# Layer two's up product with two direct pairs in place of three, and an earlier third operand split at both down products

## The chip, the cores and the metric

The kernel runs on 1 core of one Trainium2 chip. The metric is device time in microseconds (us), lower is better. A core has five engines that run their own instruction streams and wait for each other through semaphores: TensorE (matmul), VectorE, ScalarE, GpSimd, and SyncE (SP), which here only issues DMAs. 16 DMA engines move data between HBM and the on-chip memory.

## The reference, cut to what matters

One inference step of a two-layer decoder for 1024 prompt tokens and 64 sample tokens (8 sequences of 8), width 1024. Layer 1 has an attention mixer, layer 2 a pooling mixer; each layer ends with the same MLP:

```python
def _sq_relu_mlp(x, w1, w2):                 # w1 (1024, 4096), w2 (4096, 1024)
    return jnp.square(jax.nn.relu(x @ w1)) @ w2
...
xp = xp + _rms(_sq_relu_mlp(_rms(xp, gl[2]), mlp_w1[l], mlp_w2[l]), gl[3])
xs = xs + _rms(_sq_relu_mlp(_rms(xs, gl[2]), mlp_w1[l], mlp_w2[l]), gl[3])
```

Here xp are the prompt rows and xs the sample rows, l is the layer and gl its norm gains. Everything is float32. The change touches the MLPs of both layers, mostly the up product `x @ w1` of layer 2.

## The kernel before, in words

**Three passes.** TensorE takes fp32r operands, which are rounded. To keep float32 precision every operand is split in a high part (ScalarE, a copy to fp32r) and a low part (VectorE, raw minus high), and each product is made of three matmuls: high by high, high by low, low by high.

**The up product.** w1's 4096 columns are 32 tiles of 128, taken as 16 pairs (i = 0 to 15). A pair can be done in two ways. *Direct*: two tiles, each 8 row blocks by 3 passes by 3 token chunks (384, 384 and 320 wide), 72 matmuls (`up`, L1909, recorded as L1918; `up_chunk`, L1922, for the first two tiles). *By seven products* (Winograd's form of Strassen's scheme, `LateUp` for layer 2 and `SevenUp` for layer 1): P1 to P7, each 4 row blocks by 3 passes by 2 chunks of 272, 24 matmuls, in the order P1, P6, P2, P7, P5, P4, P3 (`product`, L2595, recorded as L2604), 168 a pair. The seven products need four sums of quarters of the tokens, made once (`token_sum`, `token_hi`, `token_lo`, L2878 to L2907, numbers 1 to 4, each 128 by 2176; sum 2 needs sum 1, sum 4 needs sum 2), four sums of weight quarters for each pair on GpSimd (`sum_weights`), the high and low parts of the seven weight operands (`w_split_hi`, `w_split_lo`, index q in the order of the products), and VectorE and ScalarE to take the results from PSUM (`take_out` makes U2, U3, C22, C21, C12 after P6, P7, P5, P4, P3; P7 waits for U2, P4 for U3, P3 for C22).

In layer 2 the first `FIRST` = 3 pairs (`TILES` = 6 tiles) are direct and 13 are by products. The direct tiles are there since the token sums are made while they run: `token_sum(1)` can only start when the normalised tokens have all been transposed. GpSimd adds up the first pair's weight quarters at the same time. VectorE's program is `dve_up` of `LateUp`, written out by hand, and ScalarE's is `act_up`; engines take their instructions strictly in that order. The places in PSUM go round by `bank`; `wait_place` has the waits for them.

**Between up and down.** For each pair VectorE also makes five sums of hidden rows (`combine_s`, L2485) and five of w2 rows (`combine_t`, L2499, from `one_w2`, a single buffer), which SP stores to HBM (`store_s`, `store_t`). `load_w2(i)` fills the buffer for pair i after `combine_t(i-1)`.

**The down product** is the same scheme on a larger scale: seven products M7, M1, M4, M5, M3, M2, M6, each of 8 chunks g of 24 matmuls, 512 wide (`down_part`, L1957; four of the products have 4 more for the sample rows, L1975). Chunk g's operands are loaded from HBM (`load_operands(g)`, which waits until the low parts of chunk g-2 are made, since raw buffers are two), split by ScalarE (`split_operands_hi`) and by VectorE (`split_operands_lo`, a_lo L1748 and b_lo L1751). Before the change VectorE's order at the end of the up product is: low parts of chunks 0 and 1, `combine_s(15)`, `combine_t(15)`, then low parts of chunk 2, 3, ... (with sample splits after chunk 3). SP's order is: operands 0 and 1, `store_s(14)`, operands 2, `store_t(14)`, `load_w2(15)`, operands 3, `store_s(15)`, `store_t(15)`, operands 4, ...

## Time and profile before

| | before |
|---|---|
| median of 3 runs | 2125.13 us (2122.82 to 2130.16) |
| profiled execution | 2128.65 us, span of its trace 2126.9 us |
| TensorE busy | 2048.9 us, 96% |
| VectorE busy | 1310.8 us, 62% |
| ScalarE busy | 922.2 us, 43% |
| GpSimd busy | 356.8 us, 17% |
| mean granted TensorE clock | 0.986 of 2.4 GHz |
| chain that ended last | TensorE 64%, DMA 6%, VectorE 5% |

The profile is of one execution. Its span goes from the first to the last instruction; 1.7 us of the profiled execution lie around it. An operation's time is from its start to its end, and neighbours on one engine overlap a little, so the step from start to start is the better price of one in a row. "<-DVE t_w_lo L1684" behind an operation names what the engine waited for before it; the number ahead of it is the idle time. Matmuls are pipelined: the time of one says less than that of a row of them.

### The profile page before, as it was taken

What the parts mean: (1) busy time and instruction counts of PE and PEld (TensorE: products, weight loads), DVE (VectorE), ACT (ScalarE), POOL (GpSimd) and SP (SyncE); (2) the same over time, 40 slices, a digit from 0 to 9 for tenths busy, and PEclk for the clock granted to TensorE, in tenths of its full rate; (3) what the DMA queues carried; (4) which work ended last, traced back from release to release, by engine and by line L of the source; (5) the groups of instructions that cost most, each with busy time, mean ns of one, the idle gap of its engine ahead of it and who ended that gap; (6) DMA issues with size and microseconds to landing.
All of it is one profiled execution on the core that took longest, in us unless ns stands there. A gap on an engine that the chain in (4) does not pass through costs nothing.

```text
span 2126.9 us, 34612 instructions
## 1 busy us (share of the span) xinstructions
PE 2048.9 (96%) x13923; PEld 1837.2 (86%) x13923; DVE 1310.8 (62%) x1888; ACT 922.2 (43%) x1591; POOL 356.8 (17%) x375
## 2 busy tenths in 40 slices
PE   7999999999999999999899999989999998999998
PEld 7999877777778899999788878889999997888876
DVE  5121187666556778787645467669687776444475
ACT  5111397645445444444333346454444444333343
POOL 1000131000053333331000013222232320000011
PEclk9999999999999999999999999999999999999999
DMA  5321211099522577777876542444677769664464
GB/s 168 96 74 51 101 70 35 1 355 366 160 97 84 203 260 244 258 246 285 299 252 228 165 159 97 132 135 141 208 256 243 252 223 341 230 223 160 159 221 139
DMA packets 206235, 394.39 MB, mean 185 GB/s; under 512 B 19005, under 2 KB 101109, under 8 KB 197756
## 3 DMA queue, kind: packets, MB, share of 16 engines
q1 hardware_dynamic: 199884, 387.46, 53.4%
q10 hardware_dynamic: 6192, 4.72, 0.7%
q8 instruction: 111, 1.82, 0.4%
q14 instruction: 48, 0.39, 0.1%
HBM read 273.12 MB, written 119.24 MB: 184 GB/s over the span
## 4 chain that ended last, share of the span: by engine, by line
PE 64%; DMA 6%; DVE 5%; POOL 2%; issue 2%; SPq 1%; ACT 1%; POOLq 0%; DVEq 0%; ACTq 0%
PE ps L1957 26%; PE ps L2604 25%; PE ps L4135 4%; PE ps L1975 3%; PE ps L1918 2%; DMA sa_vb_even<-cache_b_v 1%; DMA sa_vb_odd<-cache_b_v 1%; PE ps L4055 1%; DMA l_b_raw<-scratch_t_ops 1%; PE ps L1927 1%; SPq L675 1%; PE ps L4028 1%; DVE l_t_sum L2892 1%; DMA wo_raw<-attn_w_out 1%; DMA l_w_raw<-mlp_w 1%
## 5 line engine op out<-in xcount | busy, mean ns | idle before, releaser
L1957 PE MATMUL ps<-t_b_hi,t_a_hi 128*128 128x512 f32 x448 | 178.2, 398 | 7.3 <-DVE t_b_lo L1751 6.3
L1957 PE MATMUL ps<-l_b_hi,l_a_hi 128*128 128x512 f32 x448 | 175.7, 392 | 8.0 <-DVE l_b_lo L1751 7.0
L1957 PE MATMUL ps<-t_b_lo,t_a_hi 128*128 128x512 f32 x448 | 175.4, 391 | 0.0
L1957 PE MATMUL ps<-t_b_hi,t_a_lo 128*128 128x512 f32 x448 | 175.3, 391 | 0.0
L1957 PE MATMUL ps<-l_b_lo,l_a_hi 128*128 128x512 f32 x448 | 175.2, 391 | 0.0
L1957 PE MATMUL ps<-l_b_hi,l_a_lo 128*128 128x512 f32 x448 | 175.2, 391 | 0.0
L1530 POOL TENSOR_SCALAR stats<-stats 128x1 f32<-128x1 f32 x63 | 32.6, 518 | 785.7 <-ACT t_junk_y L1524 611.0
L1748 DVE TENSOR_TENSOR l_a_lo<-l_a_raw,l_a_hi 128x1024 fp32r<-128x1024 f32 x56 | 68.6, 1225 | 144.3 <-ACT l_a_hi L2634 144.3
L2634 ACT ACTIVATE l_a_hi<-l_a_raw 128x1024 fp32r<-128x1024 f32 x56 | 59.4, 1061 | 219.0 <-PE ps L1975 140.0
L1748 DVE TENSOR_TENSOR t_a_lo<-t_a_raw,t_a_hi 128x1024 fp32r<-128x1024 f32 x56 | 68.6, 1224 | 133.7 <-ACT t_a_hi L2634 133.7
L2634 ACT ACTIVATE t_a_hi<-t_a_raw 128x1024 fp32r<-128x1024 f32 x56 | 59.4, 1061 | 195.8 <-PE ps L1975 135.7
L2604 PE MATMUL ps<-u_x_sum_hi,u_w_hi 128*128 128x272 f32 x512 | 107.4, 288 | 2.7 <-DVE u_h L2466 2.7
L1957 PEld LDWEIGHTS ps<-l_b_hi,l_a_hi 128*128 128x128 f32 x448 | 84.7, 189 | 28.0 <-DVE l_b_lo L1751 7.4
L1957 PEld LDWEIGHTS ps<-t_b_hi,t_a_hi 128*128 128x128 f32 x448 | 84.8, 189 | 27.8 <-DVE t_b_lo L1751 6.7
L2604 PE MATMUL ps<-u_x_sum_lo,u_w_hi 128*128 128x272 f32 x512 | 106.9, 288 | 0.0
L1957 PEld LDWEIGHTS ps<-t_b_hi,t_a_lo 128*128 128x128 f32 x448 | 84.7, 189 | 17.9
L1957 PEld LDWEIGHTS ps<-l_b_hi,l_a_lo 128*128 128x128 f32 x448 | 84.7, 189 | 17.8
L1957 PEld LDWEIGHTS ps<-l_b_lo,l_a_hi 128*128 128x128 f32 x448 | 84.7, 189 | 17.5
L1957 PEld LDWEIGHTS ps<-t_b_lo,t_a_hi 128*128 128x128 f32 x448 | 84.9, 189 | 17.2
L985 ACT ACTIVATE pa_probs<-pa_probs,pa_least 128x257 f32<-128x257 f32 (+9 forms) x128 | 80.5, 630 | 20.2 <-DVE pa_least L1023 19.1
L2604 PE MATMUL ps<-m_xT_hi,l_w_hi 128*128 128x272 f32 x416 | 86.1, 288 | 0.0
L2604 PE MATMUL ps<-m_xT_lo,l_w_hi 128*128 128x272 f32 x416 | 85.9, 288 | 0.0
(390 smaller groups left out, 5693.3 us busy)
## 6 DMA issues: line engine op xcount, KB each, us to landing
scratch_s_ops<-u_s SPq DMA_DIRECT2D x16, 1280.0 KB, 4.8
scratch_t_ops<-u_t SPq DMA_DIRECT2D x16, 1280.0 KB, 5.7
t_a_raw<-scratch_s_ops SPq DMA_DIRECT2D x40, 512.0 KB, 3.9
t_b_raw<-scratch_t_ops SPq DMA_DIRECT2D x40, 512.0 KB, 4.8
scratch_t_ops<-l_t SPq DMA_DIRECT2D x16, 1280.0 KB, 5.5
scratch_s_ops<-l_s SPq DMA_DIRECT2D x16, 1280.0 KB, 4.6
l_a_raw<-scratch_s_ops SPq DMA_DIRECT2D x40, 512.0 KB, 3.9
l_b_raw<-scratch_t_ops SPq DMA_DIRECT2D x40, 512.0 KB, 4.8
```

The lines of the kernel that those rows point to most:

```text
L675: sp.dma_start(self.values[b % 2][:, 2 * x:2 * x + 2, :].rearrange("p e c -> p (e c)"), cache_pair(self.cache["b_v"], b, x)).then_inc(self ...
L985: nc.scalar.activation(row, row, ACT.Exp, bias=least[:, i, d:d + 1], scale=-1.0, accum_out=den[:, i, d:d + 1]).then_inc(exped, 1)
L1530: nc.gpsimd.tensor_scalar(self.ms[:, col], self.ms[:, col], EPS, None, ALU.add).then_inc(core.shifted, 1)
L1748: nc.vector.tensor_tensor(sb.a_lo[g % 3][:], sb.a_raw[:, g % 2], sb.a_hi[g % 3][:].bitcast(F32), ALU.subtract).then_inc(self.operand_lo, 1)
L1918: mm = self.nc.tensor.matmul(out, a[:, k, :], b_[:, k, c], start=(k == 0 and x == 0), stop=(k == KT - 1 and x == 2))
L1927: mm = self.nc.tensor.matmul(out, a[:, k, :], b_[:, k, c], start=(k == 0 and x == 0), stop=(k == KT - 1 and x == 2))
L1957: mm = self.nc.tensor.matmul(self.core.ps[:, self.BANK[idx] + tp, :], a[s][:, kk, tp * P:(tp + 1) * P], w[s][:, kk, :], start=(c == 0 and ...
L1975: mm = self.nc.tensor.matmul(self.core.ps[:, self.SAMPLE_BANK[idx], :], self.xT_lo[:, k % KT, first:first + P], w[s][:, kk, :], start=(k = ...
L2604: mm = self.nc.tensor.matmul(self.core.ps[:, b + j, 0:self.CHUNK], w[:, k, :], t[:, k, j * self.CHUNK:(j + 1) * self.CHUNK], start=(x in s ...
L2634: self.nc.scalar.activation(sb.a_hi[g % 3][:], sb.a_raw[:, g % 2], ACT.Copy).then_inc(self.operand_hi, 1)
L2892: sub(t[n], a, b, how).then_inc(self.x_summed_last, 1)
L4135: op = nc.tensor.matmul(out_ps(j)[:, n * 512:(n + 1) * 512], a, w[:, n * 512:(n + 1) * 512], start=(i == 0 and x == 0), stop=(i == KT - 1 ...
```

## The change

Four edits:

1. Layer 2's up product: `FIRST` from 3 to 2, so four direct tiles and 14 pairs by products. The banks of the products go round in another order (6, 4, 2, 0), the two weight buffers change places, the first product loses its wait for ScalarE's relu, and the first down chunk waits for an earlier result.
2. VectorE's and ScalarE's programs in the up head are written anew for four tiles: `split_lo(3)` right behind the first token sum, the weight parts 0 to 3 between token sums and low parts, `combine_s(1)` and `combine_t(1)` left to the first pair by products.
3. SP, both layers: `load_operands(3)` goes ahead of `load_w2(15)`.
4. VectorE, both layers: `split_operands_lo(2)` goes ahead of `combine_t(15)`; the loops that follow start from 3.

```diff
--- before.py
+++ after.py
@@ -2236,8 +2236,9 @@
                 self.load_operands(sp, 2)
             if i >= 1:
                 self.store_t(sp, i - 1)
+                if i == PAIRS - 1:
+                    self.load_operands(sp, 3)
                 self.load_w2(sp, i)
-        self.load_operands(sp, 3)
         self.store_s(sp, PAIRS - 1)
         self.store_t(sp, PAIRS - 1)
 
@@ -2567,6 +2568,7 @@
         self.split_operands_lo(dve, 1)
         for piece in range(5):
             self.combine_s(dve, PAIRS - 1, piece)
+        self.split_operands_lo(dve, 2)
         for piece in range(5):
             self.combine_t(dve, PAIRS - 1, piece)
 
@@ -2690,8 +2692,9 @@
 
 
 
-    FIRST = 3
+    FIRST = 2
     SLOTS = 5
+    PLACE_BANK = (6, 4, 2, 0)
     TILES = 2 * FIRST
     LEAD = 0
     ORDER = [(i, x) for i in range(FIRST, PAIRS) for x in (1, 6, 2, 7, 5, 4, 3)]
@@ -2718,7 +2721,7 @@
         self.x_sum[1] = [xT_hi[:, 0:k, H:], xT_lo[:, 0:k, H:]]
         self.t_sum = {n: at(f"t_sum{n}", o + lo, [P, k, H])[:] for n, o in places.items()}
         self.t_sum[1] = at("t_sum1", LateMap.TOKENS, [P, k, H])[:]
-        weights = (LateMap.WEIGHTS_EVEN, LateMap.WEIGHTS_ODD)
+        weights = (LateMap.WEIGHTS_ODD, LateMap.WEIGHTS_EVEN)
         self.w_sum = [at(f"w_sum{s}", o, [P, 3, k, P]) for s, o in enumerate(weights)]
         self.w_sum_lo = [at(f"w_sum_lo{s}", o, [P, 3, k, P], F32R) for s, o in enumerate(weights)]
         self.e1 = [at(f"w_e1_{s}", o + 6144, [P, KT, P]) for s, o in enumerate(weights)]
@@ -2821,8 +2824,9 @@
             if i == PAIRS - 1:
                 self.load_operands(sp, 2)
             self.store_t(sp, i - 1)
+            if i == PAIRS - 1:
+                self.load_operands(sp, 3)
             self.load_w2(sp, i)
-        self.load_operands(sp, 3)
         self.store_s(sp, PAIRS - 1)
         self.store_t(sp, PAIRS - 1)
 
@@ -2925,7 +2929,7 @@
 
     def act_up(self, act):
 
-        order = {1: 2, 2: 4, 3: 3}
+        order = {1: (2,), 2: (4, 3)}
         for n in range(self.TILES):
             if n + 2 < self.TILES:
                 self.split_hi(act, n + 2)
@@ -2933,41 +2937,35 @@
                 for q in range(4):
                     self.w_split_hi(act, q)
             self.hidden(act, n)
-            if n in order:
-                self.token_hi(act, order[n])
+            for x in order.get(n, ()):
+                self.token_hi(act, x)
         self.token_hi(act, 1)
         super().act_up(act)
 
     def dve_up(self, dve):
 
         self.token_sum(dve, 1)
+        self.split_lo(dve, 3)
+        self.token_sum(dve, 2)
         for piece in range(5):
             self.combine_t(dve, 0, piece)
-        self.token_sum(dve, 2)
-        self.split_lo(dve, 3)
         self.token_sum(dve, 4)
         self.token_lo(dve, 2)
-        self.split_lo(dve, 4)
+        self.token_sum(dve, 3)
+        for q in range(2):
+            self.w_split_lo(dve, q)
+        self.token_lo(dve, 4)
+        for q in range(2, 4):
+            self.w_split_lo(dve, q)
         for piece in range(5):
             self.combine_s(dve, 0, piece)
-        self.token_lo(dve, 4)
-        self.token_sum(dve, 3)
-        self.split_lo(dve, 5)
-        for piece in range(5):
-            self.combine_t(dve, 1, piece)
         self.token_lo(dve, 3)
-        for piece in range(5):
-            self.combine_s(dve, 1, piece)
-        for q in range(4):
-            self.w_split_lo(dve, q)
         self.token_lo(dve, 1)
         super().dve_up(dve)
 
     def wait_place(self, pe, i, x):
 
-        if i == self.FIRST and x == self.P1:
-            pe.wait_ge(self.relu_done, 3 * (self.TILES - 1))
-        elif i == self.FIRST and x == self.P6:
+        if i == self.FIRST and x == self.P6:
             pe.wait_ge(self.relu_done, 3 * self.TILES)
         super().wait_place(pe, i, x)
 
@@ -2992,7 +2990,7 @@
             if tp == 0:
                 pe.wait_ge(self.c11_taken, self.PAST["c11_taken"] + PAIRS - self.FIRST)
             if tp == 2:
-                pe.wait_ge(self.added, self.PAST["added"] + self.nth_added(PAIRS - 1, self.C21))
+                pe.wait_ge(self.added, self.PAST["added"] + self.nth_added(PAIRS - 2, self.C12))
         elif idx == self.M1:
             pe.wait_ge(self.added, self.PAST["added"] + 5 * (PAIRS - self.FIRST))
         else:
@@ -3869,7 +3867,7 @@
             m0.w_split_lo(dve, 7)
             m0.w_split_lo(dve, 8)
             m0.dve_up(dve)
-            for s in range(2, 40):
+            for s in range(3, 40):
                 m0.split_operands_lo(dve, s)
                 m0.down_slot(dve, s)
                 if s == 26:
@@ -3981,7 +3979,7 @@
             m1.split_lo(dve, 2)
             dve.wait_ge(x3_stored, 16 * NT)
             m1.dve_up(dve)
-            for s in range(2, 56):
+            for s in range(3, 56):
                 m1.split_operands_lo(dve, s)
                 m1.down_slot(dve, s)
                 if s == 42:
```

## Rows read from the trace of the kernel before

**Rows 1.** Chain of waits by time: start, us, what.

```profile
1016.83 40.98 PE ps L1957 x168
...
1446.65 4.11 DVE l_t L2499 x5
...
1456.75 38.94 PE ps L1918 x216
...
1505.08 6.24 PE ps L2604 x48
...
1511.36 244.25 PE ps L2604 x1944
...
1830.27 5.44 PE ps L1957 x24
```

**Rows 2.** TensorE's timeline: start, us, operation, idle time before it, releaser.

```profile
1456.75 1.27 PE L1918 MATMUL ps<-m_xT_hi,t_w_hi 128*128 128x384 f32 x3 [3.08 <-DVE t_w_lo L1684]
```

**Rows 3.** Stretches: length, busy PE, PEld, DVE, ACT, POOL, granted clock, DMA share, GB/s.

```profile
1015.00:1016.00 1.00, 0.00 (x0) 0.00 (x0) 1.00 (x2) 1.00 (x3) 0.00 (x0) 0.79 0.92 389
...
1455.00:1456.00 1.00, 0.00 (x0) 0.00 (x0) 1.00 (x2) 0.41 (x1) 0.00 (x0) 0.95 0.77 158
...
1462.00:1463.00 1.00, 1.00 (x5) 1.00 (x5) 1.00 (x1) 1.00 (x1) 0.00 (x0) 0.64 0.00 0
```

**Rows 4.** The page's costliest groups: the down product's first pass in layer 2.

```profile
L1957 PE MATMUL ps<-l_b_hi,l_a_hi 128*128 128x512 f32 x448 | 175.7, 392 | 8.0 <-DVE l_b_lo L1751 7.0
```

**Rows 5.** VectorE's timeline at the start of the down products.

```profile
1011.40 3.10 DVE L2499 TENSOR_TENSOR u_t<-u_w_raw 128x512 f32<-128x512 f32 x5 [3.93 <-DMA u_w_raw<-mlp_w]
...
1026.39 1.22 DVE L1751 TENSOR_TENSOR t_b_lo<-t_b_raw,t_b_hi 128x1024 fp32r<-128x1024 f32 x1
...
1775.27 3.19 DVE L2485 TENSOR_TENSOR l_s<-l_h 128x512 f32<-128x512 f32 x5 [0.36 <-ACT l_h L2449]
```

**Rows 6.** GpSimd's timeline in layer 2's up head.

```profile
1444.33 3.47 POOL L2262 TENSOR_TENSOR l_w_sum<-l_w_e,l_w_sum 128x512 f32<-128x512 f32 x1
```

**Rows 7.** VectorE's timeline in layer 2's up head.

```profile
1470.22 2.42 DVE L2892 TENSOR_TENSOR l_t_sum<-m_xT_hi 128x2176 f32<-128x2176 f32 x1
...
1477.50 1.23 DVE L1684 TENSOR_TENSOR t_w_lo<-t_raw,t_w_hi 128x1024 fp32r<-128x1024 f32 x1
...
1481.80 2.43 DVE L2907 TENSOR_TENSOR l_x_sum_lo<-l_t_sum,l_x_sum_hi 128x2176 fp32r<-128x2176 f32 x1
...
1484.14 3.10 DVE L2485 TENSOR_TENSOR l_s<-l_h 128x512 f32<-128x512 f32 x5
...
1487.15 0.69 DVE L2301 TENSOR_TENSOR l_w_e_lo<-l_w_e,l_w_hi 128x512 fp32r<-128x512 f32 x1
...
1504.22 0.71 DVE L2466 TENSOR_TENSOR l_h<-l_first,ps 128x544 f32<-128x544 f32 x1
```

**Rows 8.** ScalarE's timeline in layer 2's up head.

```profile
1498.13 2.01 ACT L2900 ACTIVATE m_xT_hi<-l_t_sum 128x2176 fp32r<-128x2176 f32 x1
...
1500.05 0.61 ACT L2292 ACTIVATE l_w_hi<-l_w_sum 128x512 fp32r<-128x512 f32 x1
```

**Rows 9.** ScalarE's timeline at the start of the down products.

```profile
1014.05 1.06 ACT L2634 ACTIVATE t_a_hi<-t_a_raw 128x1024 fp32r<-128x1024 f32 x1 [6.26 <-DMA t_b_raw<-scratch_t_ops]
...
1024.15 1.06 ACT L2634 ACTIVATE t_a_hi<-t_a_raw 128x1024 fp32r<-128x1024 f32 x1 [6.02 <-DMA t_b_raw<-scratch_t_ops]
...
1777.71 1.04 ACT L2635 ACTIVATE l_b_hi<-l_b_raw 128x1024 fp32r<-128x1024 f32 x1
```

**Rows 10.** SP's queue in layer 1.

```profile
1000.73 0.43 SPq L2201 DMA_DIRECT2D u_w_raw<-mlp_w  x1
...
1014.53 0.33 SPq L2205 DMA_DIRECT2D scratch_t_ops<-u_t  x1
...
1016.86 0.37 SPq L1655 DMA_DIRECT2D t_a_raw<-scratch_s_ops  x1
```

**Rows 11.** A stretch of layer 1, columns as in rows 3.

```profile
1014.05:1024.15 10.10, 7.32 (x21) 5.84 (x22) 8.62 (x10) 4.09 (x6) 0.00 (x0) 0.66 1.02 412
```

## The prediction

> **What bounds the kernel now.** The page first: TensorE is busy for 96% of the span, and the chain of waits lies on it for 64%, mostly in L1957 and L2604. A change on other engines pays only where TensorE stands still. The chain in order of time and TensorE's timeline show three such places that the change touches. All times are us from the span's start.
>
> At layer 2's up head the six direct tiles come before the pairs of seven products. Tile 3 waits for its low part, which stands in VectorE's program behind the first token sum, `combine_t(0)` and the second token sum. TensorE idles 3.08, from 1453.67 to 1456.75 [rows 1, 2]. The granted clock fell to 1.2 GHz at 1455.9, in that idle time, and came back at 1462.7 (a slice at 0.95 and one at 0.64 give the moments [rows 3]), so 6.0 of tile 3 ran at half pace and 3.0 more were lost. Tiles 3 to 5 took 38.94; less 3.0, a tile is 12.0. Product P7 of the first pair starts at 1505.08, its last four products are done 12.3 later, at 1517.4, and 1944 matmuls take 244.25 without a pause, which is 21.1 for a pair of 168 [rows 1].
>
> At each down product chunk 2 waits for its low parts: 7.0 idle in layer 2 and 6.3 in layer 1 [rows 4]. These stand behind `combine_t(15)`, which waits for the last w2 load [rows 5]. Chunk 2 starts at 1016.83, so chunk 1 ended at 1010.5. Seven chunks then take 40.98 where 168 matmuls at 5.44 for 24 take 38.1 [rows 1]: the other 2.9 is the clock, which fell 5 into the idle time, at 1015.6 [rows 3]. Layer 2 repeats it: chunk 1 ends at 1781.5, chunk 2 starts at 1788.54, seven take 40.83, and the clock fell 2 into the idle time. Chunk 4 thus starts at 1016.83 + 40.98 - 27.2 = 1030.6, and at 1788.54 + 40.83 - 27.2 = 1802.2.
>
> **The up head, VectorE.** I follow its new program from the same start, 1436.3; nothing ahead of it changes. First token sum, beside GpSimd's weight sums: to 1446.6. `split_lo(3)`: 1.1 alone. It meets GpSimd's last weight sum, which runs to 1447.8 [rows 6]; `combine_t` took 4.1 in this place against 3.1 free of it [rows 1, 5], so I add 1.0: 1448.7. That is 5 ahead of the end of tile 2, so tile 3 starts at 1453.7 at full clock and ends at 1465.7. Gain so far: 3.1 + 3.0 = 6.1.
>
> From here each step of a token sum is 2.4 (the third sum's three take 7.3), a low part 2.3 and `combine_s` 3.0, from start to next start [rows 7]. Second sum 4.8, `combine_t(0)` 3.0, fourth sum 4.8, low part of sum 2 2.3, third sum 7.3: to 1471.0. ScalarE's program has the high part of sum 3 ahead of the first weight parts: 1.9 for it, 0.6 for the weight [rows 8], 0.2 of handing over, to 1473.7. VectorE waits for that, then `w_split_lo(0)` takes 0.6 [rows 7]. The first product can start at 1474.4, and TensorE has stood idle for 8.7. This is a new wait, and what is queued behind it on VectorE is all that the next products need.
>
> VectorE goes on: `w_split_lo(1)` 0.6, low part of sum 4 2.3, two weight parts 1.2, `combine_s(0)` 3.0, low parts of sums 3 and 1 4.7, `w_split_lo(4)` 0.6, to 1486.8. Then U2 is taken, and P7 starts 0.86 after that begins, as before [rows 1, 7]: 1487.6. The three products between take 9.05 at full clock, or 12 if the first 6 run at half, and end by 1486.4: the clock falls where VectorE is later anyway. I cost that at nothing; without the cover it costs 3.0.
>
> **Sum of the up head.** P7 at 1487.6, four products 12.3, one more pair 21.1: 1521.0, against 1517.4, so 3.6 later. By its parts: two direct tiles -23.9, stall and slow clock before tile 3 -6.1, a pair +21.1, stall before P1 +8.7, from P1 to P7 +3.8 (13.2 in place of 9.4). Behind that: the next loads go out after `store_s(0)`, whose sum is ready at 1481.5; GpSimd's weight sums then run at about 1491 to 1498, beside VectorE's takes for P4 and P3. The trace has no such overlap there; the nearest row is the wait of 0.3 before P4 in the old first pair, inside the 12.3. Bounds: 0.3 less, and 1.5 more (two small operations held up by 1.0 each, less slack). I take nothing. The other end of the head: were P1 not held up, P7 would still wait for VectorE's 47.8 of work, until 1485.0, so the head can be at best 1.0 later. The new order of banks frees P1 from a wait for ScalarE's relu; P1 is later than that anyway, so it is worth nothing. Two fewer direct weight loads and the earlier bank wait of the first down chunk free only idle time.
>
> The Trainium skill (SBUF — State Buffer, "Who interferes with whom") says that a VectorE operation with two SBUF inputs and a GpSimd operation that reads SBUF exclude each other for a whole instruction. The trace shows less in this stretch: both took about 3.4 side by side, where 2.4 and 1.7 alone would add up to 4.1. By the rule `split_lo(3)` waits until 1447.8 and ends at 1449.0, not 1448.7, and the sum is 0.3 later.
>
> **The down start, both layers.** The low parts of chunk 2 now come right after `combine_s(15)`. Layer 2: `combine_s` ends at 1778.5 [rows 5], the high parts at 1778.8 [rows 9], the low parts at 1780.9, before chunk 1 ends at 1781.5. So chunk 2 starts with no wait. But what stays behind `combine_t(15)` is now chunk 3, and `combine_t` is itself later: `load_w2(15)` is moved behind `load_operands(3)`, which waits on SP for the low parts of chunk 1. The queue is full through this stretch (DMA share 1.02 at 412 GB/s [rows 11]), and transfers land in the order of issue, w2 at 1011.4 and operands 3 at 1014.05 [rows 5, 9]. So they change places: w2 lands at 1014.05, and in layer 2 at 1786.4. `combine_t` 3.1 and chunk 3's low parts 2.3 give 1019.4 and 1791.8. Chunk 2 ends at 1010.5 + 5.44 = 1015.9 and at 1786.9: new stalls of 3.5 and 4.9.
>
> Chunk 4 comes next. `load_operands(4)` is no longer held by the low parts of chunk 2 but stands on SP's queue behind `store_t(15)`, which waits for `combine_t(15)`. The store goes out at 1017.2, not 1014.53 [rows 10], and at 1789.6, not 1786.2. While the queue still has the `s` store to move, that costs nothing, and operands 4 land at 1024.15 as before [rows 9], in layer 2 at 1796.5; where it runs dry first, up to 1.0 and 1.6. I take 0.7 and 1.2. From landing to the end of the low parts was 3.46 [rows 5, 9], so chunk 4 can start at 1028.3 and 1801.2. Chunk 3, from 1019.4 and 1791.8 at a slow clock, ends by 1027.7 and 1800.0: covered. The gain is 1030.6 - 1028.3 = 2.3 in layer 1 and 1802.2 - 1801.2 = 1.0 in layer 2: of 9.2 and 9.7, most comes back as the stalls before chunks 3 and 4. Bounds: 3.0 and 2.2 if operands 4 land as before; below nothing if the clock falls twice.
>
> **Sum.** +3.6 - 2.3 - 1.0 = +0.3. The profiled execution took 2128.65 (span 2126.9); it would be 2128.95. The median of the runs is 2125.13, 3.5 below it, with 7.3 between the ends of three runs; on the median: 2125.4.
>
> **Rivals.** (1) Slower, by the clock. If the clock doesn't fall in the stall before chunk 3, chunk 3 ends at 1024.9, TensorE idles again until 1028.3, the clock falls in that second stall and chunk 4 runs slow on the path: 2.7 to 3.0 lost in each layer, which turns -3.3 into +2.4. With the overlap with GpSimd in the head (+1.5) this is +7.5: 2132.6. For it: both idle times of [rows 3], and layer 2's, were followed by a slow stretch. Against: the clock fell within 2.3 of the start in two of the three, so the first stall should take it. It decides from the point where chunk 3 runs at full clock. The Trainium skill (TensorE: Matmul & The Clock Gate, "HAM oscillation") has this as half the throttled time, paid again at each wait that is long enough; it speaks against cutting one stall in two.
>
> (2) Faster, by the queue. If latency and not bytes sets when operands 4 land, their earlier issue (by at most 1.9, from 1016.86 to 1014.95) counts, and w2 isn't delayed. Then the down starts gain 4.9 and 4.1; with +3.6 the sum is -5.4: 2119.7. Against it: the DMA share of 1.02.
>
> (3) The head does what its title says: P1 starts at tile 3's end because weight parts precede the sums. The programs as written don't do that before the third sum; it would give 2.6 at most: 2122.8.
>
> **How the numbers follow.** Forecast, within 4 of no change: 0.70. Rival 1: 0.14. Rival 2: 0.06. Rival 3: 0.05. Something else: 0.05. A measurement of this kernel can tell about 0.3% from no change, 6.4. Faster by more than that needs rival 2 and luck: 0.06; slower, most of rival 1: 0.12; within: 0.82. The range reaches past rival 2 and to most of rival 1: 2119.0 to 2132.0.
>
> **What would show it.** Right: TensorE idle 8 to 9 before the first product of layer 2's pairs and 1 to 4 before its P7; no wait at chunk 2 of either down product, 3.5 and 4.9 at chunk 3 with `b_lo` as releaser, 0 to 3 at chunk 4. Wrong: no stall before P1 (the head is off by up to 2.6), w2 landing at its old time (the swap), a slow clock in chunk 4 (rival 1).

## The result, and the profile after

The changed kernel takes 2137.51 us (median of 9 runs, 2132.52 to 2145.12), the kernel before 2125.07 on the same chip. The ratio is 1.0053, 95% interval 1.0041 to 1.0065: 11.3 us slower, between 8.7 and 13.8. Forecast was no change, with the range up to 2132.0.

The profiled execution took 2132.52 (span 2130.7), only 3.9 more than that of before. It is the fastest of its nine, and before's lies 3.6 above the median of its runs, so the two spans must not be subtracted. I compare the changed places instead: the layer 1 down product from its first matmul to its first sample matmul (L1957, L1975), layer 2's up product from tile 0 to its end, and the layer 2 down product as the first. The first and last times of these lines give them.

| us | down start, layer 1 | up, layer 2 | down start, layer 2 | sum |
|---|---|---|---|---|
| before | 58.1 | 336.6 | 58.7 | 453.4 |
| after | 60.3 | 343.0 | 57.5 | 460.8 |
| after, minus before | +2.2 | +6.4 | -1.2 | +7.4 |
| forecast | -2.3 | +3.6 | -1.0 | +0.3 |

The page's groups of after, as [rows 4]:

```profile
L1957 PE MATMUL ps<-t_b_hi,t_a_hi 128*128 128x512 f32 x448 | 178.5, 398 | 8.5 <-DVE t_b_lo L1751 7.5
L1957 PE MATMUL ps<-l_b_hi,l_a_hi 128*128 128x512 f32 x448 | 175.5, 392 | 6.5 <-DVE l_b_lo L1751 6.3
...
L2606 PE MATMUL ps<-m_xT_hi,l_w_hi 128*128 128x272 f32 x448 | 93.5, 290 | 9.9 <-DVE l_w_e_lo L2302 8.8
```

The down product waits as long as before (7.5 and 6.3, against 6.3 and 7.0), and a wait of 8.8 is new. TensorE's timeline of after has the single stalls, as [rows 2] (the idle time stands in the brackets):

```profile
1017.94 0.50 PE L1957 MATMUL ps<-t_b_hi,t_a_hi 128*128 128x512 f32 x1 [4.03 <-DVE t_b_lo L1751]
...
1028.74 0.63 PE L1957 MATMUL ps<-t_b_hi,t_a_hi 128*128 128x512 f32 x1 [3.44 <-DVE t_b_lo L1751]
...
1473.01 0.82 PE L2606 MATMUL ps<-m_xT_hi,l_w_hi 128*128 128x272 f32 x2 [8.76 <-DVE l_w_e_lo L2302]
...
1486.15 0.62 PE L2606 MATMUL ps<-l_x_sum_hi,l_w_hi 128*128 128x272 f32 x2 [2.46 <-DVE l_h L2467]
...
1498.10 0.49 PE L2606 MATMUL ps<-m_xT_hi,l_w_hi 128*128 128x272 f32 x2 [1.17 <-DVE l_h L2467]
...
1796.05 0.50 PE L1957 MATMUL ps<-l_b_hi,l_a_hi 128*128 128x512 f32 x1 [4.08 <-DVE l_b_lo L1751]
...
1805.61 0.50 PE L1957 MATMUL ps<-l_b_hi,l_a_hi 128*128 128x512 f32 x1 [2.20 <-DVE l_b_lo L1751]
```

Chunks 3 and 4 stall in both layers; in the head P1, P7 and P3. I had not forecast the last. The chain of waits of after says where it comes from:

```profile
1480.13 0.34 SPq L2791
...
1481.94 1.25 SPq L2182
...
1483.24 7.39 DMA l_w_e<-mlp_w
...
1490.79 1.29 POOL l_w_sum L2258
...
1494.69 1.25 POOL l_w_sum L2263
...
1496.03 0.10 DVE l_w_e_lo L2302
...
1497.24 0.73 DVE l_h L2467
```

SP issues the store of `combine_s(0)` (L2791) and only then the weight loads of the second pair. They land at 1490.63, GpSimd's four sums run to 1495.94, and then comes a step of VectorE that I had not seen. Its timeline:

```profile
1445.15 2.31 DVE L1684 TENSOR_TENSOR t_w_lo<-t_raw,t_w_hi 128x1024 fp32r<-128x1024 f32 x1
...
1485.29 0.72 DVE L2467 TENSOR_TENSOR l_h<-l_first,ps 128x544 f32<-128x544 f32 x1
...
1496.03 0.69 DVE L2302 TENSOR_TENSOR l_w_e_lo<-l_w_e,l_w_hi 128x512 fp32r<-128x512 f32 x1 [4.35 <-POOL l_w_sum L2263]
...
1497.24 0.72 DVE L2467 TENSOR_TENSOR l_h<-l_h,ps 128x544 f32<-128x544 f32 x1
```

`w_split_lo(7)`, the low part of the second pair's P1, uses raw weights and no sum. But it overwrites them in place, so it waits until GpSimd has read them for all four sums. It stands ahead of the take of C22 (1497.24), and P3 waits for C22.

The clock, in stretches of after (columns as in rows 3):

```profile
1015.00:1016.00 1.00, 0.00 (x0) 0.00 (x0) 1.00 (x3) 0.00 (x0) 0.00 (x0) 1.00 0.23 88
...
1020.00:1021.00 1.00, 1.00 (x4) 0.78 (x3) 0.97 (x2) 0.00 (x0) 0.00 (x0) 0.50 0.55 166
...
1030.00:1031.00 1.00, 1.00 (x4) 0.79 (x3) 1.00 (x2) 0.91 (x2) 0.00 (x0) 0.50 0.66 168
...
1487.00:1488.00 1.00, 1.00 (x6) 1.00 (x6) 0.87 (x2) 0.91 (x2) 0.00 (x0) 0.50 1.15 348
```

It is at 1.2 GHz after chunk 3's stall, again after chunk 4's in layer 1, and again after P7's. In the first row the DMA queue moves 88 GB/s: it has run dry, since SP issued nothing between 1006.3 and 1015.64.

### The profile page after: what moved, and what is told of

Read it like the earlier page. It is cut to its first block and busy times, and to the rows that moved or that the text cites. A ratio compares the mean times of both kernels' runs of the same rounds, so it can differ in the third digit from the quotient of the medians.

```text
span 2130.7 us, 34702 instructions
## 1 busy us (share of the span) xinstructions
PE 2042.7 (96%) x13947; PEld 1831.3 (86%) x13947; DVE 1321.3 (62%) x1898; ACT 926.9 (44%) x1593; POOL 362.2 (17%) x380
## 5 line engine op out<-in xcount | busy, mean ns | idle before, releaser
L1957 PE MATMUL ps<-t_b_hi,t_a_hi 128*128 128x512 f32 x448 | 178.5, 398 | 8.5 <-DVE t_b_lo L1751 7.5
L1957 PE MATMUL ps<-l_b_hi,l_a_hi 128*128 128x512 f32 x448 | 175.5, 392 | 6.5 <-DVE l_b_lo L1751 6.3
L1957 PE MATMUL ps<-t_b_lo,t_a_hi 128*128 128x512 f32 x448 | 175.8, 393 | 0.0
L1957 PE MATMUL ps<-t_b_hi,t_a_lo 128*128 128x512 f32 x448 | 175.5, 392 | 0.0
L1957 PE MATMUL ps<-l_b_lo,l_a_hi 128*128 128x512 f32 x448 | 175.0, 391 | 0.0
L1957 PE MATMUL ps<-l_b_hi,l_a_lo 128*128 128x512 f32 x448 | 174.9, 390 | 0.0
L1957 PEld LDWEIGHTS ps<-t_b_hi,t_a_hi 128*128 128x128 f32 x448 | 84.8, 189 | 29.5 <-DVE t_b_lo L1751 8.3
L1957 PEld LDWEIGHTS ps<-l_b_hi,l_a_hi 128*128 128x128 f32 x448 | 84.5, 189 | 26.8 <-DVE l_b_lo L1751 7.1
L2606 PE MATMUL ps<-m_xT_hi,l_w_hi 128*128 128x272 f32 x448 | 93.5, 290 | 9.9 <-DVE l_w_e_lo L2302 8.8
L1957 PEld LDWEIGHTS ps<-t_b_hi,t_a_lo 128*128 128x128 f32 x448 | 85.0, 190 | 18.1
L1957 PEld LDWEIGHTS ps<-l_b_hi,l_a_lo 128*128 128x128 f32 x448 | 84.5, 189 | 17.8
L1957 PEld LDWEIGHTS ps<-t_b_lo,t_a_hi 128*128 128x128 f32 x448 | 84.9, 189 | 17.2
L1957 PEld LDWEIGHTS ps<-l_b_lo,l_a_hi 128*128 128x128 f32 x448 | 84.4, 188 | 17.4
L2606 PE MATMUL ps<-m_xT_lo,l_w_hi 128*128 128x272 f32 x448 | 93.0, 289 | 0.0
```

The lines of the kernel that those rows point to most:

```text
L1957: mm = self.nc.tensor.matmul(self.core.ps[:, self.BANK[idx] + tp, :], a[s][:, kk, tp * P:(tp + 1) * P], w[s][:, kk, :], start=(c == 0 and ...
L2606: mm = self.nc.tensor.matmul(self.core.ps[:, b + j, 0:self.CHUNK], w[:, k, :], t[:, k, j * self.CHUNK:(j + 1) * self.CHUNK], start=(x in s ...
```

## The experiments

A ratio of 1.001 is 2.1 us. "In the trace" is the sum of the three changed places less before's 453.4; "measured" is the timed ratio.

| kernel | in the trace | measured (95%) |
|---|---|---|
| changed | +7.4 | +11.3 (+8.7 to +13.8) |
| changed, second profile | +6.6 | |
| down edits alone | +0.5 | +3.8 (+0.4 to +7.0) |
| head alone | +6.2 | +8.5 (+5.7 to +11.3) |
| second loads first | +10.5 | +11.9 (+8.3 to +15.3) |
| weights first | +5.3 | +8.1 (+4.9 to +11.1) |
| early low part, three pairs | -3.2 | -3.4 (-5.7 to -1.1) |
| late w2 sums, three pairs | -5.7 | -6.4 (-9.4 to -3.2) |
| take before split | +6.4 | +4.9 (+1.9 to +7.9) |
| down, VectorE edit alone | +0.3 | -1.3 (-4.0 to +1.7) |
| operands first, three pairs | -8.4 | -8.5 (-11.7 to -5.1) |
| both fixes, three pairs | -10.3 | -10.8 (-14.7 to -7.2) |
| two pairs, eased program | +1.4 | +3.0 (0.0 to +6.2) |

The trace's figure lies inside the interval for every kernel but the changed one, where it is 1.3 short of its lower end. The places left out take 1669 to 1681 us in these traces, in no order that goes with an edit.

Two cautions. First, one trace is one execution. Where a place is not edited, it still varies: the head with three direct pairs and the old order takes 336.6, 335.5, 335.5, 336.6 and 335.4 in five traces, the old down start 58.1, 57.1 and 58.5 in layer 1 and 58.7, 57.8 and 59.4 in layer 2. A difference of 1 us between two rows therefore says nothing. Second, "down edits alone", "head alone", "second loads first" and "weights first" were timed on another chip than the runs below them, each against the kernel before on its own chip. A difference of two timed rows across that line can hold a difference of the chips.

### The two halves of the change

Before with edits 3 and 4 only, and the changed kernel with these two undone.

> The kernel before with the down edits alone (operands 3 ahead of the last w2 load on SP, low parts of chunk 2 ahead of combine_t(15), both layers). Theory A, the head holds the loss: the two down starts cancel, as in the one trace of the changed kernel (chunk 4 ran 1.6 us later in layer 1, 1.6 us earlier in layer 2, counted from the end of chunk 1), so within 2.5 us of before. Theory B, the down starts hold it because chunk 4 now stalls too and the clock falls twice in each: 5 to 8 us slower than before. The prediction's own sum would be 3.3 us faster.

> The changed kernel with the down edits undone, so two direct pairs and the new programs of the up head alone. Theory A: the head loses the 3.6 us of the prediction and 2.7 more, the stall before P3 that the trace of the changed kernel shows, plus the slow clock after the stall before P7, so 6 to 12 us slower than before. Theory B: 3 to 5 us slower.

The head gives +6.2 in the trace and +8.5 timed, as theory A had it (6 to 12); the down edits give +0.5 and +3.8. They add up. The 3.8 lies between the two theories on the down starts (within 2.5, or 5 to 8), and its interval reaches into both; the trace is on the side of the first. The down edits alone show the changed kernel's stalls, 4.20 and 3.47 in layer 1, 4.44 and 1.69 in layer 2: so they owe nothing to the new head. They bring +2.4 in layer 1 and -0.8 in layer 2. In the trace of the head alone the waits are shared out otherwise than in the changed kernel: 1.42 before P7 with the clock at 2.4 GHz behind it, and 3.08 before P3 with 3.4 us at 1.2 GHz behind it. The head takes 344.7 there.

### The second pair's loads first

```diff
                 self.load_w2(sp, i + 1)
+                sp.wait_ge(self.up_ready, self.TILES)
+                self.load_e0(sp, first + 1)
+                self.load_e1(sp, first + 1)
                 self.store_s(sp, i)
-        sp.wait_ge(self.up_ready, self.TILES)
-        self.load_e0(sp, first + 1)
-        self.load_e1(sp, first + 1)
```

> The changed kernel with the weight loads of the second pair ahead of store_s(0) on SP's queue, so that they go out when the fourth tile ends and not after combine_s(0). If the stall before the first pair's P3 comes from VectorE waiting in w_split_lo(7) for GpSimd's weight sums, and these for late loads, that stall goes and the time falls by 2 to 4 us against the changed kernel. The rival: GpSimd's sums now run beside VectorE's token sums and low parts and slow those (they took 3.4 us side by side where 2.4 alone), P7 comes 3 us later and the time stays or rises by up to 2 us.

The stall before P3 is gone, and nothing is won. TensorE's timeline, and then VectorE's and GpSimd's:

```profile
1480.89 0.82 PE L2606 MATMUL ps<-m_xT_hi,l_w_hi 128*128 128x272 f32 x2 [9.35 <-DVE l_w_e_lo L2302]
...
1496.22 0.49 PE L2606 MATMUL ps<-l_x_sum_hi,l_w_hi 128*128 128x272 f32 x2 [3.41 <-DVE l_h L2467]
```

```profile
1482.45 3.50 DVE L2911 TENSOR_TENSOR l_x_sum_lo<-l_t_sum,l_x_sum_hi 128x2176 fp32r<-128x2176 f32 x1
...
1481.94 1.73 POOL L2263 TENSOR_TENSOR l_w_sum<-l_w_e,l_w_sum 128x512 f32<-128x512 f32 x1
```

GpSimd's sums now fall into VectorE's work between P1 and P7. The low part of sum 4 takes 3.50 in place of 2.42, a weight part 1.76 in place of 0.69, and P7 is 15.3 behind P1, not 13.1. The rival of the expectation holds: in the stretch where VectorE is the bound, GpSimd costs what it saves later. The head is 344.2 against 343.0. The rest of the +10.5 lies in layer 2's down start (59.2 against 57.5), which this edit doesn't touch.

### The weight parts ahead of the third token sum

`w_split_hi(0..3)` on ScalarE ahead of the high parts of sums 4 and 3, and on VectorE:

```diff
-        self.token_sum(dve, 3)
         for q in range(2):
             self.w_split_lo(dve, q)
+        self.token_sum(dve, 3)
         self.token_lo(dve, 4)
```

> The changed kernel with the four high weight parts on ScalarE ahead of the high parts of sums 4 and 3, and the two low weight parts on VectorE ahead of the third token sum. The stall of 8.8 us before P1 goes. If VectorE's whole work up to U2 sets the head, P7 moves by only the 2.6 us that VectorE waited, and a stall of 6 to 9 us appears before P7 (or before P6 or P2, at a low part) in its place: 2 to 4 us faster than the changed kernel. If the stall before P1 is itself the cost, 8 us or more faster.

```profile
1472.10 0.79 PE L2606 MATMUL ps<-l_x_sum_hi,l_w_hi 128*128 128x272 f32 x2 [6.93 <-ACT l_h_sample L2848]
...
1481.36 0.49 PE L2606 MATMUL ps<-l_x_sum_hi,l_w_hi 128*128 128x272 f32 x2 [0.67 <-DVE l_h L2467]
...
1493.64 0.49 PE L2606 MATMUL ps<-m_xT_hi,l_w_hi 128*128 128x272 f32 x2 [3.03 <-DVE l_h L2467]
```

Timed, this is 3.2 better than the changed kernel, inside the expected 2 to 4, but in the trace the head is only 0.9 shorter. P1 starts at tile 3's end, and P6 waits 6.9 for ScalarE's relu of tile 3, which stands behind the high part of sum 3. P7 comes 51.2 behind tile 0, not 53.9: 2.7 earlier, the 2.6 that VectorE had waited. But P3 now waits 3.03, not 1.17, with a slow clock behind it (1494.3 to 1497.6), which takes most of it back. VectorE's work up to P7 was the bound, as expected, and not the stall before P1. Another 1.5 of the trace's gain is layer 1's down start, where the edit does nothing. There a stall of 2.47 before chunk 4 was followed by full clock, the only stall above 2.27 in the down starts and heads of these traces that was:

```profile
1028.26 0.50 PE L1957 MATMUL ps<-t_b_hi,t_a_hi 128*128 128x512 f32 x1 [2.47 <-DVE t_b_lo L1751]
...
1029.00:1030.00 1.00, 1.00 (x6) 0.78 (x6) 1.00 (x2) 1.00 (x3) 0.00 (x0) 1.00 0.68 70
```

### The take of C22 ahead of the in-place low part

VectorE's step 4 makes no weight part, step 5 takes C22 and then makes parts 7 and 8.

> The changed kernel with one move on VectorE: the low part of the eighth weight operand (which waits for all of GpSimd's sums of the second pair) behind the take of C22, not ahead of it. Theory (that wait holds up C22, so TensorE idles ahead of P3 and its clock falls there): no idle time ahead of P3, 1.1 to 2.6 us faster than the changed kernel, so 8.7 to 10.2 slower than the kernel before. Rival (the clock falls anyway, from the stalls before P1 and P7): under 0.5 us of difference in the head.

```profile
1474.04 0.82 PE L2606 MATMUL ps<-m_xT_hi,l_w_hi 128*128 128x272 f32 x2 [8.78 <-DVE l_w_e_lo L2302]
...
1487.19 0.49 PE L2606 MATMUL ps<-l_x_sum_hi,l_w_hi 128*128 128x272 f32 x2 [1.07 <-DVE l_h L2467]
```

No wait before P3. The head takes 339.9, not 343.0: 3.1 less, of which 1.2 is that wait and the rest the slow stretch behind P7, which is missing too. P7 still comes 13.15 after P1, but with 1.07 of idle time ahead of it, since the products before it ran at half pace until 1480.3 (6.2 behind P1, in the changed kernel 3.1); after 1.07 the clock stayed at 2.4 GHz. So 1.2 is owed to the edit, and the rest to where the clock happened to come back. Timed, it is 6.4 better than the changed kernel, so the expected 8.7 to 10.2 over before was too much: +4.9. The sum of the three places is only 1.0 below the changed kernel's, since layer 2's down start is 1.7 longer here. Where the other 5 of the timed difference come from isn't shown.

### Two direct pairs with an eased program

The last two edits together, and the low part of sum 1 behind the take of U2.

> The changed kernel with its head's three waits eased: weight parts 0 to 3 of the first product ahead of the third token sum on both engines, the low part of token sum 1 behind the take of U2, the low part of the eighth weight operand behind the take of C22. Theory (VectorE's 47.8 of work up to P7 is what two direct pairs can't cover, so even a better order wins at most 1 or 2): P1 without a wait, P6 held to about 1476, P7 at 1483 in place of 1487.6, no wait before P3; 5 to 8 faster than the changed kernel, still 2 to 6 slower than the kernel before. Rival (only the order was wrong, not the count of direct tiles): no slower than the kernel with both down edits alone, ratio 1.002 or below.

The head takes 336.3, against 336.6 before and 343.0 changed: TensorE waits 6.93 once, before P6, and nowhere after, up to the down product. Timed, it is +3.0, inside the expected 2 to 6, but the rival's mark (a ratio of 1.002 or below, no slower than the down edits alone) is met too: 1.0014, and +3.0 against +3.8. The head's trace is on the rival's side. The order made the loss, and the count of direct tiles costs nothing that can be seen; this order gains nothing either, and no other was tried. My bound in the prediction ("at best 1.0 later") was passed by 1.3: it counted 47.8 of VectorE's work ahead of P7, and here the low part of sum 1, 2.4 of it, stands behind the take of U2.

### The low part of tile 3, with three direct pairs

```diff
         self.token_sum(dve, 1)
+        self.split_lo(dve, 3)
         for piece in range(5):
             self.combine_t(dve, 0, piece)
         self.token_sum(dve, 2)
-        self.split_lo(dve, 3)
```

> The kernel before with one move on VectorE in layer 2's up head: the low part of tile 3 right behind the first token sum, ahead of the first w2 sums and the second token sum (nothing else, three direct pairs stay). Theory (the stall of 3.1 ahead of tile 3 and the 3.0 of slow clock behind it are on the path, and nothing else waits for VectorE's order there): no idle time ahead of tile 3, clock full through the direct tiles, later work of VectorE covered; 6 us faster than the kernel before. Rival (VectorE's program to the first P7 has no slack, or tile 4 stalls in its place): tile 4's or 5's low part comes late by as much, the gain is below 2.

A gain of 3.4 of the 6.1 (4.3 in the head's trace), between the theory's 6 and the rival's 2. The stall and slow clock at tile 3 are gone, but VectorE's program is full: tile 5 waits for its low part by 1.36, and P7 by 0.68. Neither is followed by a slow clock. 4.3 and these 2.0 come to 6.3, so the price of 6.1 was right. The slow clock at tile 3 was also dearer in before's profile than in most: it came back 6.0 behind the stall's end there, but 3.7 to 3.8 behind it in three of the four other traces with that stall.

### The down start: VectorE's edit alone

> The kernel before with the down edit on VectorE alone (low parts of chunk 2 ahead of the last w2 sums), SP's order as before: w2 lands ahead of operands 3. Theory (w2 and operands 3 change places in a full queue): w2 lands at 1011.4 as before, operands 3 at 1014; chunk 3 stalls by 2 to 3 in place of 3.5 to 4.1, the store of w2 sums and operands 4 go out 1.5 to 2 earlier than with both edits, so chunk 4 waits less; 2 to 6 us faster than the kernel with both down edits. Rival (the clock decides, it falls in whichever stall comes): same stalls within 1, no difference.

```profile
1020.15 0.50 PE L1957 MATMUL ps<-t_b_hi,t_a_hi 128*128 128x512 f32 x1 [1.75 <-DVE t_b_lo L1751]
...
1031.17 0.79 PE L1957 MATMUL ps<-t_b_hi,t_a_hi 128*128 128x512 f32 x1 [5.29 <-DVE t_b_lo L1751]
```

Chunk 3 stalls less, as expected, since operands 3 and w2 stand in another order; chunk 4 stalls more (5.29 against 3.44), but only because chunk 3 is done earlier. Operands 4 land 25.8 behind the product's start, with both down edits 28.0, and chunk 4 begins 29.3 and 31.5 behind it. So in layer 1 the swap of w2 and operands 3 costs 2.0 (down start 58.5 against 60.5). In layer 2 it is the other way round (58.6 against 57.9), and in the table's +0.3 the head, which neither run edits, hides the difference (336.6 against 335.5). Timed, this kernel is 5.1 better than with both down edits, as the theory had it, but the two were timed on different chips and their intervals overlap. The traces show 1.3 of the 5 in the two down starts; the rest stays open.

### The down start: the w2 sums late

Low parts of chunks 2 and 3 ahead of `combine_t(15)`; SP's order operands 3, w2, `s`, operands 4, 5, `t`. Then once more, with operands 4 ahead of the `s` store:

```diff
+        self.load_operands(sp, 4)
         self.store_s(sp, PAIRS - 1)
-        self.load_operands(sp, 4)
         self.load_operands(sp, 5)
         self.store_t(sp, PAIRS - 1)
```

> The kernel before with another down start in both layers: low parts of chunks 2 and 3 ahead of the last w2 sums on VectorE, and on SP operands 3 ahead of the last w2 load, operands 4 and 5 ahead of the last store of w2 sums. Theory (each stall at a down start is VectorE's program order or the DMA queue's order, the change only moved it from chunk 2 to chunks 3 and 4, each time with a slow clock behind it): no wait over 1 us at chunks 2 to 5, no slow clock, 8 to 9 us gained in each layer, 15 to 18 together. Rival (the DMA queue is full and sets the pace, the bytes can't land in time whatever the order): stalls of 2 to 4 us stay at chunks 3 to 5 and the gain is below 6.

> The kernel before with the down start of the run on late w2 sums, but operands 4 on SP ahead of the last store of hidden sums (order: operands 3, last w2 load, operands 4, store of hidden sums, operands 5, store of w2 sums). Theory (the queue is full from 1005 to 1027, so what stands ahead of operands 4 in bytes sets chunk 4's stall of 4.6): operands 4 land 1.79 MB earlier, 4.4 us at 412 GB/s, no stall over 1 at chunks 2 to 5, no slow clock; 4.6 + 4.8 of stalls and some 4 of slow clock less than the run on late w2 sums had, so 14 to 18 us faster than the kernel before. Rival (another chunk or another wait takes the stall's place): under 9 us faster than the kernel before.

TensorE's timeline of the first, a stretch of it in which operands 4 are under way, and the timeline of the second:

```profile
1027.28 0.79 PE L1957 MATMUL ps<-t_b_hi,t_a_hi 128*128 128x512 f32 x1 [4.64 <-DVE t_b_lo L1751]
...
1011.00:1023.78 12.78, 11.63 (x52) 9.30 (x50) 9.00 (x12) 4.09 (x7) 0.00 (x0) 1.00 1.04 406
```

```profile
1033.05 0.79 PE L1957 MATMUL ps<-t_b_hi,t_a_hi 128*128 128x512 f32 x1 [3.21 <-DVE t_b_lo L1751]
...
1799.86 0.50 PE L1957 MATMUL ps<-l_b_hi,l_a_hi 128*128 128x512 f32 x1 [3.06 <-DVE l_b_lo L1751]
```

One stall per layer in place of the changed kernel's two, before chunk 4 in both runs (4.64 and 4.84 in the first, 3.21 and 3.06 in the second), each with a slow stretch. In the first run the bytes set it: the queue moves 406 GB/s without a gap, VectorE is idle ahead of operands 4 and makes their low parts as soon as ScalarE has made the high ones. In the second run 1.79 MB fewer stand ahead of operands 4, and in layer 1 they land 18.7 behind the product's start, not 23.1: 4.4 earlier, just as expected. The stall shrinks by only 1.4 and 1.8, because now VectorE's order is in the way. Its timeline in the second run, layer 1, where operands 4 land at 1026.26:

```profile
1023.96 3.09 DVE L2502 TENSOR_TENSOR u_t<-u_w_raw 128x512 f32<-128x512 f32 x5
1026.98 2.49 DVE L1788 TENSOR_TENSOR m_xT_lo<-u_h_sample,m_xT_lo 128x512 fp32r<-128x512 f32 x4
1029.50 1.23 DVE L1769 TENSOR_TENSOR u_h_sample<-u_h_sample 128x1024 f32<-128x1024 f32 x1
1030.64 1.22 DVE L1748 TENSOR_TENSOR t_a_lo<-t_a_raw,t_a_hi 128x1024 fp32r<-128x1024 f32 x1
```

`combine_t(15)` and the sample splits stand ahead of chunk 4's low parts, and VectorE has no idle time between 1021.7 and 1033.0. Chunk 3 was done at 1029.84. ScalarE has the high parts ready by 1028.3, so with the low parts right behind them chunk 4 could have started some 3 earlier (an estimate from these rows; no run tried it). Both runs gained less than I expected: 6.4, not 15 to 18, and 8.5, not 14 to 18. In the first the rival holds, that bytes set the pace. In the second the rival of its own expectation holds: another wait takes the stall's place.

### Both fixes with three direct pairs

> The kernel before (three direct pairs) with the early low part of tile 3 and the down start with operands first. Theory (the two places are independent): the sum of the two, 17 to 24 us faster than the kernel before. Rival (VectorE or the queue couples them): less than the larger of the two alone plus 1.

The two places are nearly independent: 3.4 and 8.5 give 11.9, measured 10.8, at a median of 2114.97; in the traces 3.2 and 8.4 give 11.6, measured 10.3. The rival's 9.5 at most lies inside the timed interval, so a small coupling isn't excluded. The gain is less than the 17 I expected, as each part was. It beats both kernels.

### The changed kernel, once more

> The changed kernel as it is, for another profile of it: its first profile was taken of its fastest execution, 5 below its median. Theory (the granted clock falls after some short stalls in some executions and not in others): an execution near 2137 shows a slow stretch, or a longer wait, at a place of the up head or the down starts where the first profile had none, and the rest of the trace agrees within 1. Rival (executions differ outside the changed places): the head from tile 3 to the end of the up product takes 343 again and the difference lies elsewhere.

This execution took 2134.99. Head 343.1, down starts 59.9 and 57.0: within 0.5 of the first profile, and the other 3 us lie outside of the changed places. The rival holds: executions differ elsewhere, and one span says nothing on 5 us.

## Why the prediction was wrong, point by point

In the trace the sum is 7.1 above the forecast: 2.8 behind P7, 4.5 in layer 1's down start, less 0.2 in layer 2's. What failed is a wait that I didn't follow (P3), the clock behind two stalls that I forecast but didn't price (P7, chunk 4 of layer 1), and the landing of operands 4 in layer 1.

**The head up to P7: right.** Tile 0 starts at 1432.3, 1.5 ahead of before's. With that shift I had P1 at 1472.9 and P7 at 1486.1; they started at 1473.01 and 1486.15. The stall of 8.7 measured 8.76. `split_lo(3)` took 2.31 beside GpSimd's sum, 1.1 more than alone, where I had added 1.0. The slow clock behind P1's stall was hidden. The Trainium skill's exclusion rule (SBUF — State Buffer, "Who interferes with whom"), which would have made it 0.3 more, can't be told apart here. One reading beside it was wrong: I took 1.7 for GpSimd's weight sum alone, but that row lies beside work of VectorE. With VectorE idle it takes 1.28 in the trace of after, so 2.4 and 1.3 one after the other give 3.7, against the 3.4 of both side by side.

**Behind P7: the step that failed.** I wrote "Bounds: 0.3 less, and 1.5 more … I take nothing". From P7's start to the end of the up product (1775.3 by the last time of its line) 289.15 went by; before took 265.3 (1505.08 [rows 1] to 1770.4), and with one more pair, 21.1, 286.4 was due. Of the 2.8, 1.2 is the stall before P3. I had timed GpSimd's sums right, at 1491 to 1498, but asked only whether they slow VectorE's takes, not who waits for them. The in-place low part does, and the run with the take first shows it: with the take of C22 ahead of that part the wait before P3 is gone. The other 1.6 is the clock: P7's stall of 2.46 was followed by 3.4 at half pace (from 1486 on slices at 0.68, 0.50, 0.50 and 0.62; 3.4 at half pace lose 1.7). I had forecast 1 to 4 of idle time there and put no price on its clock. With these, +3.6 becomes +6.4, as measured. In the run with the head alone the same two terms are shared out otherwise (3.08 before P3 and the slow stretch behind that) and make 4.5.

**The down start, layer 1: wrong by 4.5.** Seen from the product's start, chunk 3 began at 20.5 (forecast 19.9) and chunk 4 at 31.3 (forecast 28.8; 31.1 before). Between them lies operands 4's landing: 27.8 after the start, where I took 24.65 + 0.7, so 2.5 too early. The failed step is "where it runs dry first, up to 1.0": against before they land 3.2 later. SP held the queue for `combine_t(15)` until 1015.64; all that was issued had landed by then (DMA share 0.23), and behind the restart two slices moved at only 215 and 166 GB/s (1019 to 1021). The other part is the clock. It fell behind the stall before chunk 3 (at 1018.7), came back at 1022.1, and fell again behind the stall before chunk 4 (at 1029.0): 3.4 at half pace, 1.7 lost. The first slow stretch cost nothing, since chunk 3 was done before operands 4 had landed. This has the outcome of rival 1, but not its condition and not its price: rival 1 let chunk 3 run at full clock and put 2.7 to 3.0 on the second fall. My argument against it, that the first stall takes the fall, doesn't exclude a second one. I had given it 0.14 in both layers together; the second fall came in layer 1 here and in both layers in three runs (second loads first, take before split, eased program). The Trainium skill (TensorE: Matmul & The Clock Gate, "HAM oscillation") has half the throttled time as the loss, paid again at each wait that is long enough; the trace agrees, with 1.7 of 3.4 lost and the second fall 10.3 us behind the first.

**Layer 2: right, with some luck.** -1.2 against -1.0; chunk 4 began 30.1 behind the product's start, forecast 30.7. But the same down code gave 57.0 to 59.2 in seven traces and the old one 57.8 to 59.4 in three: the means, 58.2 and 58.6, differ by 0.4.

**Against the clock on the wall.** The terms sum to +7.4, timed it is 8.7 at least. Some of it is that this execution had luck in layer 2: its idle 2.20 before chunk 4 was followed by full clock, and the same 2.20 in the run with the take first was not. Stretches of that run, then of after, each from a little behind that stall:

```profile
1805.00:1806.00 1.00, 1.00 (x3) 0.77 (x3) 1.00 (x2) 0.83 (x2) 0.00 (x0) 0.50 0.56 174
```

```profile
1806.00:1807.00 1.00, 1.00 (x6) 0.82 (x5) 1.00 (x2) 1.00 (x2) 0.00 (x0) 1.00 0.38 43
```

That is 1.7 in some executions; the second profile showed no fall there either. The larger part is on the other side, before's single profile. Over all traces that share the code of a place, the head takes 343.6 (three traces) against 335.9 (five), layer 1's down start 60.1 (seven) against 57.9 (three), layer 2's 58.2 (seven) against 58.6 (three). By these means the change costs 7.7 + 2.2 - 0.4 = 9.5, inside the timed 8.7 to 13.8. What lies between 9.5 and 11.3 the runs can't resolve.

**Rivals 2 and 3.** Operands 4 landed later, not earlier, so rival 2 is out; and in the run with operands first 1.79 MB fewer ahead of them brought them 4.4 earlier, the time of these bytes at 412 GB/s. P1 did wait for the third sum, so rival 3 is out; in the run with the weight parts first, where P1 doesn't wait for it, P6 waits instead.

## What to carry to other kernels

For each operation that a change delays, list who waits for it, and count a buffer that is overwritten in place as a wait for all its readers. A stall that is cut in two can cost its clock twice, so price each stall on its own with the slow stretch behind it. Where a stall ends on a full DMA queue, reorder the bytes first, with stores behind the loads that the matmuls need next; then read the engine's program again, since once the bytes come early enough, what stands ahead of the splits there is the next wait. Look at each chunk behind the first until the work is ahead again. And before a difference of one or two us is read out of two traces, compare the same place in traces that don't change it.

## What the runs showed of the hardware

- Idle times of TensorE and the clock behind them, in the down starts and the up heads of all 14 traces: of thirteen between 0.45 and 1.75 none was followed by a slow clock; of four at 2.20 to 2.27, two were; of three at 2.46 and 2.47, two; all 51 from 2.51 to 9.35 were. The clock came back 3.0 to 6.4 us behind the end of the idle time. So a stall of 2.5 can cost 1.7 more (3.4 at half pace).
- The length of the idle time alone doesn't decide it. Ahead of the up head every trace has two idle times of 2.46 or 2.47, 8.6 to 10.2 us apart. The second was followed by a slow clock in all 14 traces, the first in only five (before's among them, not the changed kernel's). That is 1.7 of the difference in the places left out, and no edit's doing.
- The fall may lie in the idle time or up to 1.5 us behind its end, on work that has already resumed (chunk 4 of layer 1: work from 1028.74, slow from 1029.0).
- In the down start the queue moved 406 GB/s in a full stretch. In after it ran dry at 1015; behind the restart it moved 328 to 399 GB/s for three slices and then 215 and 166 for two.
- In the profile of the run with operands first the granted clock stood at 0.95 where all other profiles have 1.00, yet the matmuls kept their pace: 443 of the down product between 1100 and 1200 in this trace and in that of the late w2 sums. So the record of 0.95 is not what makes its span of 2125.7 longer than the median of its runs, 2116.62; its places left out are the longest (1680.7).
- Operations side by side on VectorE and GpSimd both stretch: 3.50 for 2.42, and 1.73 for 1.28.
